# Sums of squares in an encoder's projection: two rounded matmuls and a GpSimd subtraction in place of one fp32 matmul

## The reference

```
h = rmsnorm(x, norm1_g)
proj = h @ w_in
...
y = b_gate * depthwise_conv_centred(c_gate * h, conv_w)
y = rmsnorm(y in 8 groups of 64 channels)
...
qkv = silu(depthwise_conv_centred(qkv, conv_w))
q = l2norm(q per head of 128) * 128 ** -0.5
k = l2norm(k per head of 128)
```

## Time and profile before

| what | value |
|---|---|
| time, median of 3 runs | 2924.35 us (2923.51 to 2928.12) |
| the profiled execution's own time | 2924.2 us |
| its span, first to last instruction | 2922.5 us |
| TensorE busy (matmul), share of the span | 2623.8 us, 90% |
| GpSimd busy | 1202.9 us, 41% |
| mean granted clock of TensorE | 0.945 |

### The profile page before, as it was taken

One profiled execution on the slowest core, in us unless ns is written; L12 is line 12 of the kernel. 1 busy time (PEld: TensorE's weight loads), 2 busy tenths in 40 slices (PEclk: granted clock), 3 DMA queues, 4 the chain that ended last, 5 costly groups with the idle time before them and its releaser, 6 DMA issues. The chain is left out here.

```text
span 2922.5 us, 44609 instructions
## 1 busy us (share of the span) xinstructions
PE 2623.8 (90%) x14924; PEld 2308.0 (79%) x14925; DVE 1845.5 (63%) x2218; ACT 980.8 (34%) x2064; POOL 1202.9 (41%) x879
## 2 busy tenths in 40 slices
PE   4999999999986999999979994698999999999980
PEld 3998998998974899999968883586787888878770
DVE  6356465564562777777753335979867766687773
ACT  6044153252352343433422221132233333333323
POOL 3111100100103667576632221466656665666660
PEclk6999999999997999999989996799999999999995
DMA  5021111111113222222124445389578677787777
GB/s 166 10 75 50 37 58 42 45 58 34 52 46 87 66 63 80 66 61 78 30 96 149 147 149 202 105 297 334 163 231 291 226 232 228 241 301 231 236 252 273
DMA packets 223041, 408.19 MB, mean 140 GB/s; under 512 B 14408, under 2 KB 103736, under 8 KB 222904
## 3 DMA queue, kind: packets, MB, share of 16 engines
q1 hardware_dynamic: 207624, 350.91, 34.5%
q0 software_dynamic: 15296, 55.59, 8.1%
HBM read 326.01 MB, written 80.44 MB: 139 GB/s over the span
## 5 line engine op out<-in xcount | busy, mean ns | idle before, releaser
L467 PE MATMUL project_proj<-hT_high,project_w_high 128*128 128x412 f32 (+3 forms) x1392 | 496.1, 356 | 29.3 <-issue 10.7
L467 PE MATMUL project_proj<-hT_low,project_w_high 128*128 128x412 f32 (+3 forms) x1392 | 474.5, 341 | 0.0
L467 PE MATMUL project_proj<-hT_high,project_w_low 128*128 128x412 f32 (+3 forms) x1392 | 474.3, 341 | 0.0
L1833 PE MATMUL experts_h<-experts_w_high,experts_xT_high 128*128 x832 | 339.2, 408 | 20.4 <-DVE experts_w_low L1733 12.4
L1733 DVE TENSOR_TENSOR experts_w_low<-experts_w_whole,experts_w_high 128x2048 fp32r<-128x2048 f32 x128 | 335.1, 2618 | 4.4
L1833 PE MATMUL experts_h<-experts_w_low,experts_xT_high 128*128 x832 | 334.3, 402 | 0.0
L1833 PE MATMUL experts_h<-experts_w_high,experts_xT_low 128*128 x832 | 329.2, 396 | 0.0
L467 PEld LDWEIGHTS project_proj<-hT_high,project_w_high 128*128 128x128 f32 (+1 forms) x1392 | 261.1, 188 | 46.0 <-issue 31.9
L444 POOL CAST project_w_high<-project_w_whole 128x1024 fp32r<-128x1024 f32 x28 | 30.2, 1079 | 634.2 <-DMA project_w_whole<-in_w_tiles_dram 634.2
L467 PEld LDWEIGHTS project_proj<-hT_low,project_w_high 128*128 128x128 f32 (+1 forms) x1392 | 261.2, 188 | 14.3 <-issue 9.6
L1731 DVE CAST experts_w_high<-experts_w_whole 128x2048 fp32r<-128x2048 f32 x128 | 198.0, 1546 | 115.9 <-DMA experts_w_whole<-in_w_dram 115.6
(11 more groups left out here) (292 smaller groups left out, 5363.1 us busy)
## 6 DMA issues: line engine op xcount, KB each, us to landing
experts_w_whole<-in_w_dram SPq DMA_DIRECT2D x128, 1024.0 KB, 8.9
experts_w_whole<-in_w_dram SPq DMA_DIRECT2D x32, 2048.0 KB, 13.8
delta_qkv<-feat SPq DMA_DIRECT2D x36, 768.0 KB, 5.0
project_w_whole<-in_w_tiles_dram SPq DMA_DIRECT2D x28, 512.0 KB, 4.3
feat<-project_out SPq DMA_DIRECT2D x48, 205.0 KB, 1.9
x_rows<-output_x SPq DMA_DIRECT2D x19, 512.0 KB, 6.4
xn_rows<-output_xn SPq DMA_DIRECT2D x19, 512.0 KB, 6.4
normalise_x<-in_x_dram SPq DMA_DIRECT2D x18, 512.0 KB, 3.6
```

The source lines that it names most:

```text
L467: r = pe.matmul(dst, w[s][:, kt, 0:m], x[:, kt, lo:hi], start=kt == 0 and i == 0, stop=kt == KD - 1 and i == 2)
L1833: m = pe.matmul(out[:, :], x[p][:, kt, :], w, start=kt == 0 and i == 0, stop=kt == KD - 1 and i == 2)
```

## The change

Each sum of squares is formed from two matmuls in the rounded type. ScalarE squares the chunk twice, once in fp32 and once into a rounded tile; GpSimd subtracts the rounded square from the fp32 one, in place, and TensorE adds the rounded part and the remainder into the same bank. The two weight matrices of ones become tiles of the rounded type; chunks of odd width are taken one column wider. GpSimd's order is written out anew, with the 18 subtractions between the splits. In the k stretch, SiLU and square of k stand ahead of fetching v. The tile for the norms lies in a buffer that is free at that time.

```
     def square(j, c, g):
-        act.activation(sq[:, 0:cols], o[:, 0:cols], ACT.Square).then_inc(squared, 1)
+        act.activation(sq[:, 0:cols], o[:, 0:cols], ACT.Square)
+        act.activation(sq_high[:, 0:cols], o[:, 0:cols], ACT.Square).then_inc(squared, 1)
...
+    def squares_low(j, c, g):
+        n, cols = norm_no(j, c), even(geometry(c)[3])
+        pool.wait_ge(squared, g * NORMS + (n + 1))
+        pool.tensor_tensor(sq_low[:, 0:cols], sq[:, 0:cols], sq_high[:, 0:cols].bitcast(F32), ALU.subtract).then_inc(sq_split, 1)
+
+    def iteration(g, more):
+        for c in range(NC - 1):
+            squares_low("b", c, g)
+        split("z", g, g * 7 + 5)
+        squares_low("b", NC - 1, g)
+        split("k", g, g * 7 + 6)
+        split("v", g, g * 7 + 7)
+        for c in range(NC):
+            squares_low("q", c, g)
+        if more:
+            split("q", g + 1, g * 7 + 8)
+            split("c", g + 1, g * 7 + 9)
+        for c in range(NC - 1):
+            squares_low("k", c, g)
+        if more:
+            split("h", g + 1, g * 7 + 10)
+        squares_low("k", NC - 1, g)
+        if more:
+            split("b", g + 1, g * 7 + 11)
...
     def sums(j, c, g):
-        pe.wait_ge(squared, g * NORMS + (n + 1))
+        pe.wait_ge(sq_split, g * NORMS + (n + 1))
         pe.wait_ge(nfree[n % 2], g * (NORMS // 2) + (n // 2 + 1))
         weights = k["group"] if j == "b" else k["ones"]
-        pe.matmul(nbank[n % 2][:, 0:cols], weights[:, :], sq[:, 0:cols], start=True, stop=True).then_inc(nready[n % 2], 1)
+        pe.matmul(nbank[n % 2][:, 0:cols], weights[:, :], sq_high[:, 0:cols], start=True, stop=False)
+        pe.matmul(nbank[n % 2][:, 0:cols], weights[:, :], sq_low[:, 0:cols], start=False, stop=True).then_inc(nready[n % 2], 1)
...
         for c in range(NC):
             to_raw("k", c, g)
             roots(*(("k", c - 1) if c else ("q", NC - 1)), g)
-            to_raw("v", c, g)
             silu("k", c, g)
             square("k", c, g)
+            to_raw("v", c, g)
             silu("v", c, g)
...
     @block.vector
     def _(dve):
+        for o in out:
+            dve.memset(o[:, :], 0.0)
```

More of the change, by code:

```diff
@@ L134, in masks @@
 def masks(pool, k, set0, sel):
-    fills = [(k["ones"], 1.0), (k["tri"], 1.0), (k["neg"], 0.0), (k["lower"], 1.0), (k["group"], 1.0), (k["lvl"], 0.0),
+    fills = [(k["tri"], 1.0), (k["neg"], 0.0), (k["lower"], 1.0), (k["lvl"], 0.0),
              (k["block8"], 1.0)]
@@ L141, in masks @@
     pool.wait_ge(set0, n)
-    halves = k["group"][:, :].rearrange("p (b r) -> p b r", b=2)
+    halves = k["lower"][:, :].rearrange("p (b r) -> p b r", b=2)
     eighths = k["block8"][:, :].rearrange("p (b r) -> p b r", r=8)
@@ L151, in masks @@
                            pattern=[[w, P // w], [0, w]], channel_multiplier=-1).then_inc(sel, 1)
+    pool.wait_ge(sel, 4)
+    pool.tensor_copy(k["group"][:, :], k["lower"][:, :]).then_inc(sel, 1)
+    pool.wait_ge(sel, 5)
+    pool.memset(k["lower"][:, :], 1.0).then_inc(set0, 1)
+    pool.wait_ge(set0, n + 1)
+    pool.tensor_copy(k["ones"][:, :], k["lower"][:, :])
+    n += 1
     levels = [(1 << l, d, k["lvl"][:, d, l - BASE, :].rearrange("p (b h r) -> p b h r", h=2, r=1 << l)[:, :, 1 - d, :])
@@ L160, in masks @@
                            pattern=[[-2 * s, P // (2 * s)], [0, s]], channel_multiplier=1).then_inc(sel, 1)
-    pool.wait_ge(sel, len(levels) + 4)
+    pool.wait_ge(sel, len(levels) + 5)
     for s, d, v in levels:
@@ L184, in masks @@
                                pattern=[[0, HEADS], [sign, 8]], channel_multiplier=1).then_inc(sel, 1)
-        pool.wait_ge(sel, len(levels) + 4 + 2 * (b + 1))
+        pool.wait_ge(sel, len(levels) + 5 + 2 * (b + 1))
 def normalise(nc, k, dram, hT):
@@ L298, in _, with project @@
             masks(pool, k, filled, selected)
-def project(nc, k, dram, hT, feat, ab_rows):
+def project(nc, k, dram, hT, feat, ab_rows, lg):
     with ExitStack() as ctx:
@@ L317, in project @@
         raw, out, side = ring("raw", 2), ring("out", 4), ring("side", 2)
-        sq, nrm = b.sb("squares", [P, CW]), b.sb("norms", [P, CW])
+        (sq,), (sq_low,) = over(nc, b, ("squares",), [P, CW])
+        sq_high, nrm = b.sb("squares_high", [P, CW], F32R), lg[:, :, :].rearrange("p t c -> p (t c)")
         primer, zero = b.sb("primer", [P, CONV_TILES]), b.sb("zero", [P, 1])
@@ L326, in project @@
         stored, side_stored = sems("stored", 4), sems("side_stored", 2)
-        w_high, chain, convolved, silued, squared, inverted, normed, begun, cleared, ab_set = (b.sem(n) for n in
-            "w_high conv_taps convolved silued squared inverted normed splits_begun zero_cleared ab_set".split())
+        w_high, chain, convolved, silued, squared, sq_split, inverted, normed, begun, cleared, ab_set = (b.sem(n) for n in
+            "w_high conv_taps convolved silued squared squares_split inverted normed splits_begun zero_cleared ab_set".split())
         block = ctx.enter_context(nc.Block())
@@ L341, in item, with even @@
             return {"b": c, "q": NC + c, "k": 2 * NC + 2 * c, "v": 2 * NC + 2 * c + 1}[j]
+        def even(n):
+            return n + n % 2
         def norm_no(j, c):
@@ L450, in _ @@
             with pool.Fori(0, G - 1) as g:
[L451 to L456, removed]
+                iteration(g, True)
+            iteration(G - 1, False)
             pool.wait_ge(w_loaded[3], 16 * (G + 1))
@@ L545, in square @@
             def square(j, c, g):
-                cols, o = geometry(c)[3], out[item(j, c) % 4]
+                cols, o = even(geometry(c)[3]), out[item(j, c) % 4]
                 if j == "b":
@@ L701, in _ @@
                 pe.matmul(pg[d][:, 0], k["tri"][:, d, :], gg[:, d], start=True, stop=True, skip_group_check=True)
-                pe.matmul(pg[d][:, 1], k["ones"][:, :], gg[:, d], start=False, stop=True, skip_group_check=True).then_inc(sums, 1)
+                pe.matmul(pg[d][:, 1], k["ones"][:, :].bitcast(F32), gg[:, d], start=False, stop=True, skip_group_check=True).then_inc(sums, 1)
             for d in range(2):
@@ L1506, in _ @@
                 pe.matmul(rank[h][:, :, :], k["lower"][:, :], both[:, h * H:(h + 1) * H, :], start=True, stop=True)
-                m = pe.matmul(tot[h][:, :, :], k["ones"][:, :], both[:, h * H:(h + 1) * H, :], start=True, stop=True)
+                m = pe.matmul(tot[h][:, :, :], k["ones"][:, :].bitcast(F32), both[:, h * H:(h + 1) * H, :], start=True, stop=True)
             m.then_inc(pe_s, 1)
@@ L2009, in encoder @@
         u = Bufs(nc, until_routed)
-        k["ones"], k["lower"], lg = u.sb("ones", [P, P]), u.sb("lower", [P, P]), u.sb("lg", [P, NT, NG + NE])
+        k["ones"], k["lower"], lg = u.sb("ones", [P, P], F32R), u.sb("lower", [P, P]), u.sb("lg", [P, NT, NG + NE])
         with ExitStack() as mixers:
@@ L2013, in encoder @@
             k.update({
-                "group": m.sb("group", [P, P]), "tri": m.sb("tri", [P, 2, P]), "neg": m.sb("neg", [P, 2, P]),
+                "group": m.sb("group", [P, P], F32R), "tri": m.sb("tri", [P, 2, P]), "neg": m.sb("neg", [P, 2, P]),
                 "lvl": m.sb("lvl", [P, 2, LEVELS - BASE, P]),
@@ L2028, in encoder @@
                 with nc.cleanup_on_exit():
-                    project(nc, k, dram, hT, feat, ab_rows)
+                    project(nc, k, dram, hT, feat, ab_rows, lg)
             gates = m.sb("gates", [P, 2, NT, 3 * HEADS])
```

## The result

The changed kernel takes **2950.34 us** (median of 4 runs, 2944.64 to 2960.01), the kernel before in the same comparison 2926.23 (4 runs, 2923.51 to 2929.50): a ratio of 1.0085, with a 95% interval of 1.0056 to 1.0115. It is slower by 24.1 us. The prediction said 2943.7, range 2927 to 2960, slower at 0.83.

A forecast was written before the change was run, and what follows sets the result against it. The projection was taken as bound by TensorE, busy 797 of 842 us. Groups 1 to 3 lose 18.2, the last gains 1.2: net 17.0 lost, plus 2.5 for the clock, 19.5 on 2924.2: 2943.7 us, range 2927 to 2960.

The forecast's parts named there:

- three signs of being wrong: Wrong if k0's sum starts under 19 us after q4's, k5's under 16 after chunk 3's, or 410-column subtraction under 0.8.
- TensorE's arithmetic: At every sum: two rounded matmuls cost 0.38 us instead of 0.69; 20.8 us saved in all if nothing waits.
- The longer way: Second square, GpSimd subtraction and hand-offs: a sum starts at least 1.73 us after the first square, 1.26 for chunk 5.
- b4, b5: Sums of job b, chunks 4 and 5: pair set at 0 a group, between -0.8 and +0.9 us.
- q0 to q3: Sums of job q, chunks 0 to 3: lateness slightly outweighs the 0.31 saved, -0.25 us a group.
- q4: Sum of job q, chunk 4: TensorE already waits for the square; loss 1.6 us a group.
- k0: Sum of job k, chunk 0: subtraction behind splits of next q and c; 3.3 us later in groups 1 to 3.
- The clock: After k0's pauses in three groups: half the group-end excess, 0.8 us each, 2.5 in all, bounds 0 and 5.0.
- k5: Sum of job k, chunk 5: subtraction behind the split of next h; 3.2 us later in groups 1 to 3.
- one place only: Rival: only one of the two places, k0 or k5, has its sum held by a split; 2933 us, chance 0.10.
- neither place: Rival: splits hold the sum at neither k0 nor k5, all groups go as the last; 2919.4 us, chance 0.08.
- the port: Rival: 48 subtractions of q and k slow VectorE through the shared port; 26 us more, 2970 us, chance 0.07.

The follow-up runs named there:

- e2: Changed kernel with k0's subtraction moved ahead of the splits of the next q and c on GpSimd: 2935.85 us, 1.0031 of the kernel before.
- e3: Changed kernel with k5's subtraction moved ahead of the split of the next h on GpSimd: 2937.03 us, 1.0042 of the kernel before.
- e4: Changed kernel with the edits of e2 and e3 together: 2923.90 us, 0.9993 of the kernel before.
- e6: Changed kernel without the remainder: one rounded square, one rounded matmul a sum, no subtraction: 2891.41 us, 0.9876 of the kernel before.
- e5: Kernel before with only SiLU and square of k moved ahead of fetching v: 2918.27 us, 0.9975 of the kernel before.
- e7: Kernel before plus 72 GpSimd subtractions on constants, in the change's places and order, nobody waiting for them: 2924.40 us, 0.9996.
- e1: The changed kernel run again, unedited, as yardstick: 2949.06 us, 1.0080 of the kernel before.
- e9: e4 with rounded matmul pairs only at b0 to b4 and k0 to k4, other sums one fp32 matmul: 2909.76 us, 0.9945 of the kernel before.
- e10: Changed kernel with fetching v again ahead of SiLU and square of k: 2954.48 us, 1.0102 of the kernel before.

## Why the prediction was right, and where its sizes were off

The direction and the mechanism were right, and the two places named are the cause: e2 and e3 remove one each, e4 both, and nothing of the loss against before remains. None of the three signs of being wrong appeared: k0's sum starts 21.3 to 22.0 us after q4's in groups 1 to 3, k5's 18.3 to 18.6 after k3's, and the long subtraction takes 1.05. By the prediction's steps:

- **TensorE's arithmetic.** Forecast 0.38 a sum; measured 0.38. e6 shows that it turns into time where the input is early.
- **The longer way.** Forecast 1.73 us behind the first square; measured 1.68 at q4. The subtraction takes 1.05 to 1.08 alone at 410 columns, by the line through the earlier trace rows 1.08. The Trainium skill (GPSIMD Engine Reference, 3.1 Elementwise) gave, in proportion to its width, an estimate of 0.90; the rows were the nearer.
- **b0 to b3**: gain 1.2 forecast, 1.26 from b0's to b4's sum. Right.
- **b4, b5**: set at 0. The pair, to q0's sum, gave 0.23 of loss in groups 1 and 3, 3.9 in group 2, outside the bounds, and 0.8 in the last. In group 2 a convolution step of b5 on VectorE (L657, 256 columns) took 2.50 us beside a split's subtraction on GpSimd, where such a step (L655 in group 1) takes 0.48; TensorE then idled 2.26 and went on at a granted clock of 0.64. Before, b4 to b5 was stretched in one group of four, in e5 and e7 in none, but in e6, which has no subtraction of squares on GpSimd, in two. It varies from execution to execution and is the largest part of what I can't assign to the change.
- **q0 to q3**: -0.25 forecast; 0.01 gained from q0's to q3's sum. Right: the saving and the lateness cancel. **q4**: 1.6 forecast; q3 to q4 grew by 1.36, and 1.36 + 0.31 saved = 1.67.
- **k0**: 3.3 forecast a group; q4 to k0 grew by 4.23, 4.42 and 3.73. This is the mis-sized term. In group 1 the split of q started 12.57 us behind q4's sum (219.17 - 206.60), where I had 12.2, with the loads 0.3 earlier than before; they were not earlier. The two splits took 7.95 us to their end, 224.56 + 2.56 = 227.12, where I had 7.4. From there to the sum it took 1.27, as forecast (1.26). So 0.9 is missing, and all of it lies ahead of the subtraction. It is not the same everywhere: in e1 the three groups grew by 4.24, 3.29 and 4.25. In the last group, with no split, it took 17.06 against 17.0.
- **The clock.** I took half of the excess, 0.8 a pause. From k0's to k1's sum the groups took 1.64, 1.47 and 1.67 more than the last one's 9.44: 4.8 in place of 2.5. A pause of 4.55 us pays the full price of a group's end; after q4's 1.72 the next 4.9 us ran at 1.00 in this profile. The Trainium skill (TensorE: Matmul & The Clock Gate, HAM oscillation) would have had all three pauses pay; the trace agrees with it, and the better choice was the upper bound.
- **k5**: 3.2 forecast; from k3's to k5's sum 18.61, 18.26 and 18.32 against 14.95, so 3.66, 3.31 and 3.37; the last group 14.82 against 14.8. **k1 to k3**: 0.64 gained over two steps, as forecast.

Sizing these anew from the profile of after, k0 adds 2.5, the clock 2.3 and k5 0.7 to the forecast loss of 19.5: 25.0, where the medians differ by 24.1. That profile is 9.7 us above its median, so the closeness is in part luck. In e1, whose profiled execution is the median, the same sizing adds 1.9 for k0, 3.5 for the clock and nothing for k5: 24.9. So k0's wait and the clock behind it were too small in both, and k5's size was right within what varies. Neither sum is a closed account, since b4 and b5 (5.1 more than before in after, 3.2 in e1) and the later stages stand beside it. And 2958 as the upper end of the forecast's own range is less than its listed bounds add up to, 2943.7 + 18.8 = 2962.5; the result lies inside either.

The forecast took the new order of k as part of the bundle and so did not see that it alone would gain 7.5. At k5 the longer way takes back what the order gives: from k3's to k5's sum 14.82 in the last group of after, 13.14 in e5.

Of the rivals, neither "one place only" nor "neither place" came; the subtraction is not short; the port does not carry the loss (e7).

What stays open: e4 and e9 still lose some in the first three groups at the end of the k stretch (k3 to k4 8.21, k4 to k5 7.75, against 7.73 and 7.09 in the last). There a subtraction of GpSimd takes 1.35 us and a VectorE step beside it (L653) 1.13 instead of 0.43 alone, as e4's timeline shows, GpSimd and VectorE in turn:

```profile
257.65 1.35 POOL L462 TENSOR_TENSOR project_squares_low<-project_squares_whole,project_squares_high 128x410 fp32r<-128x410 f32 x1 [7.54 <-ACT project_squares_high L586]
```

```profile
258.10 1.13 DVE L653 TENSOR_SCALAR project_out<-project_raw,cw_qkv 128x409 f32<-128x409 f32 x1
```

No run took this collision away, so it is read and not shown to be what makes k4 late.

## What to carry to other kernels

An engine that is mostly idle can still be the slow link: look at what stands ahead of a small urgent instruction in its in-order queue, above all when that is a large one that itself waits for a transfer, and put the urgent one first. A cheaper pass that needs a longer way to its input pays only at the places where the input is early by more than that way; sort the places by their slack and change those alone, as the mixed version does but for k4. Try each part of a bundled change by itself: here one moved line was worth 7.5 us, and the rest of the bundle had hidden it.

## What the runs showed of the hardware that I had not expected

- A wait of TensorE costs more than its length when it is long: 4.55 us idle were followed by 4.7 us at a granted clock of 0.69, and from k0's to k1's sum 1.5 to 1.7 us were lost again (2.9 in e1's first group). Shorter pauses cost this in some groups and not in others: q4's 1.72 us were followed by 1.00 in 21 of 24 groups (after, e1 to e4, e10), and by about 0.65, with 1.5 us lost, in three (one each in e2, e3 and e10); b5's 2.25 to 2.37 us by 0.64 to 0.69 in five of seven and by 1.00 in two.
- GpSimd and VectorE stretch each other step by step when they coincide (1.35 for 1.05 to 1.08, 1.13 for 0.43, 2.50 for 0.48), and yet 72 such subtractions, with VectorE busy 12.5 us longer, left the kernel's time as it was (e7, 0.9996).
- A wait further on swallows part of what is lost ahead of it: undoing k's order in e10 cost 3.3 us from k1's to k5's sum in the last group, and 0.8 to 1.8 in the groups where the split of h holds k5's sum.
